# Block sums of the weights of the last projection: adding DMAs from memory instead of VectorE

## What is computed

```python
def swiglu_ffn(h, w_ffn_in, w_ffn_out):
    gate, up = jnp.split(h @ w_ffn_in, 2, axis=-1)
    return (jax.nn.silu(gate) * up) @ w_ffn_out
```

## Time and profile before

| what | value |
|---|---|
| device time, median of 3 runs | 1336.9 us (1336.31 to 1337.07) |
| span of the profiled execution | 1334.3 us |
| PE busy | 1314.1 us, 98% of the span |
| DVE busy | 983.0 us, 74% |
| ACT busy | 553.2 us, 41% |
| granted PE clock, mean | 0.998 of full speed |
| weight loads (SP) | 119 of 1024 KB, 5.0 us from issue to landing in the middle |

### The profile page before, as it was taken

How to read it: one execution, slowest core, us unless ns; L and a number is a source line. 1 busy time by engine, 2 the same in 40 slices (tenths; PEclk the granted TensorE clock), 3 DMA queues, 4 the chain that set the end, 5 groups by cost and what they waited for, 6 DMA issues and landing times.

```text
span 1334.3 us, 15752 instructions
## 1 busy us (share of the span) xinstructions
PE 1314.1 (98%) x6395; PEld 1065.0 (80%) x6395; DVE 983.0 (74%) x1218; ACT 553.2 (41%) x767; POOL 87.9 (7%) x153
## 2 busy tenths in 40 slices
PE   7999999999999999999999999999999999999997
PEld 4799688778888888888788777778878888888886
DVE  4787877989778777777759799866795444446988
ACT  4553444344333333232332566774443222224543
POOL 0000000000001000100000011000002120000001
PEclk9999999999999999999999999999999999999999
DMA  9543056325455556654232211122204333225565
GB/s 391 195 136 133 4 170 207 125 81 187 158 173 176 183 162 206 221 203 163 87 106 95 88 65 46 56 95 95 95 32 156 115 116 105 98 103 199 192 221 195
DMA packets 34472, 188.01 MB, mean 141 GB/s; under 512 B 4304, under 2 KB 5088, under 8 KB 18016
## 3 DMA queue, kind: packets, MB, share of 16 engines
q1 hardware_dynamic: 20976, 140.32, 29.7%
q0 software_dynamic: 13424, 46.69, 11.0%
HBM read 182.79 MB, written 4.20 MB: 140 GB/s over the span
## 4 chain that ended last, share of the span: by engine, by line
PE 84%; DVE 8%; ACT 3%; DMA 3%; issue 2%; SPq 0%; DVEq 0%; ACTq 0%
PE bank L1678 25%; PE bank L1680 24%; PE bank L1679 24%; PE bank L2017 2%; PE bank L2018 2%; PE bank L2023 2%; DVE WL L938 2%; DMA raw<-weights 1%; PE bank L1883 1%; DMA adaf<-ada 1%; DVE ada_acc L980 1%; PE bank L2213 1%; ACT WH L448 1%; PE bank L2183 1%; PE bank L2201 1%
## 5 line engine op out<-in xcount | busy, mean ns | idle before, releaser
L1678 PE MATMUL bank<-hH,WH 128*128 128x512 f32 x992 | 390.1, 393 | 0.8 <-DVE WL L938 0.5
L1680 PE MATMUL bank<-hH,WL 128*128 128x512 f32 x992 | 386.4, 390 | 0.0
L1679 PE MATMUL bank<-hL,WH 128*128 128x512 f32 x992 | 386.2, 389 | 0.0
L938 DVE TENSOR_TENSOR WL<-raw,WH 128x2048 fp32r<-128x2048 f32 (+1 forms) x114 | 253.5, 2226 | 153.9 <-ACT WH L448 153.9
L448 ACT ACTIVATE WH<-raw 128x2048 fp32r<-128x2048 f32 (+1 forms) x117 | 218.0, 1865 | 237.4 <-DMA raw<-weights 180.0
L1678 PEld LDWEIGHTS bank<-hH,WH 128*128 128x128 f32 x992 | 186.3, 188 | 42.6 <-issue 3.3
L1680 PEld LDWEIGHTS bank<-hH,WL 128*128 128x128 f32 x992 | 186.2, 188 | 39.2
L1679 PEld LDWEIGHTS bank<-hL,WH 128*128 128x128 f32 x992 | 186.4, 188 | 37.7 <-issue 0.2
L980 DVE SCALAR_TENSOR_TENSOR ada_acc<-ada_half,csil,ada_acc 128x1024 f32<-128x1024 f32 x70 | 89.6, 1280 | 5.6 <-DMA ada_half<-ada_later 3.0
L1427 DVE SCALAR_TENSOR_TENSOR cacc<-uT,vec,cacc 128x511 f32<-128x511 f32 (+29 forms) x120 | 83.2, 753 | 0.0
L401 POOL DMA_DIRECT2D ada_half<-ada_later x80 | 42.4, 530 | 570.7 <-DVE ada_acc L980 335.1
(11 more groups left out here) (358 smaller groups left out, 2147.3 us busy)
## 6 DMA issues: line engine op xcount, KB each, us to landing
raw<-weights SPq DMA_DIRECT2D x119, 1024.0 KB, 5.0
ada_half<-ada_later POOLq DMA_DIRECT2D x80, 512.0 KB, 4.5
adaf<-ada SPq DMA_DIRECT2D x8, 1024.0 KB, 19.9
xT<-x_t SPq DMA_DIRECT2D x4, 512.0 KB, 5.8
x_rows<-xB POOLq DMA_DIRECT2D x32, 64.0 KB, 2.2
gF<-x_rows POOLq DMA_DIRECT2D x3, 512.0 KB, 6.9
ctxT<-ctx_t SPq DMA_DIRECT2D x1, 1024.0 KB, 28.3
out_t<-gF SPq DMA_DIRECT2D x2, 512.0 KB, 2.6
```

The source lines that it names most:

```text
L938: TT_(lo_of(c, 0, width), raw_of(c, 0, width), hi_of(c, 0, width), sub).then_inc(s.lo_done, 1)
L1678: mm(o, lh, rh, start=start, stop=False, skip_group_check=skip)
L1679: mm(o, lh, rl, start=False, stop=False, skip_group_check=skip)
L1680: return mm(o, ll, rh, start=False, stop=stop, skip_group_check=skip)
```

## The change

The block sums that are plain additions move into DMAs that POOL issues. Such a DMA reads weights from memory and adds them to what lies in the `raw` tile (`accum_op=add`).

- First pass: A21 += A22 is now such a DMA of 256 KB (`add_block`). A12 = A11 - A22 stays on DVE.
- Second pass: SP loads only the first three blocks, 768 KB. A21 += A11 is a DMA of 256 KB, and A11 += A12 with A12 += A22 is one of 512 KB (`add_rows`). DVE does no sums here.
- POOL issues a chunk's adds once its load has landed and the adds of the chunk two before have landed. ACT's `split_hi` waits for the adds (semaphores `ada_in`), and in the first pass for DVE's difference as well.
- The adds stand on POOL ahead of the four `x_rows` loads.

```diff
+def added_up_to(c):
+    return 16 * (STEPS // 2 + sum(1 if x < C_REST else 2 for x in range(C_DOWN2, c + 1) if (x - c) % 2 == 0))
...
             def load_chunk(c):
                 sp.wait_ge(s.mm_done, 16 * freed_by(c) + 16)
-                sp.dma_start(raw_of(c), weights[c if c < C_REST else c - PAIRED]).then_inc(raw_in[slot_of(c)], 16)
+                if c < C_REST:
+                    sp.dma_start(raw_of(c), weights[c]).then_inc(raw_in[slot_of(c)], 16)
+                else:
+                    sp.dma_start(raw_of(c, 0, 3 * CW), weights[c - PAIRED, :, 0:3 * CW]).then_inc(raw_in[slot_of(c)], 16)
...
+            def add_block(c, to, of):
+                pool.dma_start(raw_of(c, CW * to, CW * to + CW), weights[c if c < C_REST else c - PAIRED, :, CW * of:CW * of + CW],
+                               accum_op=add).then_inc(ada_in[c % 2], 16)
+
+            def add_rows(c):
+                src = weights[c - PAIRED, :, CW * W_A12:CW * W_A22 + CW].rearrange("p (b j) -> p b j", j=CW)
+                pool.dma_start(quarters(c, 0, 3, 2), src, accum_op=add).then_inc(ada_in[c % 2], 16)
+
+            for c in range(C_DOWN2, N_LOADS):
+                pool.wait_ge(raw_in[slot_of(c)], 16 * loads_up_to(c))
+                if c >= C_DOWN2 + 2:
+                    pool.wait_ge(ada_in[c % 2], added_up_to(c - 2))
+                if c < C_REST:
+                    add_block(c, W_A21, W_A22)
+                else:
+                    add_block(c, W_A21, W_A11)
+                    add_rows(c)
             pool.wait_ge(s.mm_done, 16 * freed_by(N_LOADS - 1) + 16)
...
             def split_hi(c, width=CH):
                 if c >= C_DOWN2:
-                    act.wait_ge(s.w_sum, 2 * (c - C_DOWN2) + 2)
+                    if c < C_REST:
+                        act.wait_ge(s.w_sum, c - C_DOWN2 + 1)
+                    act.wait_ge(ada_in[c % 2], added_up_to(c))
...
             def weight_sums(c):
                 dve.wait_ge(raw_in[slot_of(c)], 16 * loads_up_to(c))
-                a11, a21 = raw_of(c, CW * W_A11, CW * W_A11 + CW), raw_of(c, CW * W_A21, CW * W_A21 + CW)
-                a12, a22 = raw_of(c, CW * W_A12, CW * W_A12 + CW), raw_of(c, CW * W_A22, CW * W_A22 + CW)
-                if c < C_REST:
-                    TT_(a21, a21, a22, add).then_inc(s.w_sum, 1)
-                    TT_(a12, a11, a22, sub).then_inc(s.w_sum, 1)
-                else:
-                    TT_(a21, a21, a11, add).then_inc(s.w_sum, 1)
-                    dve.wait_ge(s.w_sum, 2 * (c - C_DOWN2) + 1)
-                    TT_(quarters(c, 0, 3, 2), quarters(c, 0, 3, 2), quarters(c, 2, 4), add).then_inc(s.w_sum, 1)
+                a11, a12 = raw_of(c, CW * W_A11, CW * W_A11 + CW), raw_of(c, CW * W_A12, CW * W_A12 + CW)
+                TT_(a12, a11, raw_of(c, CW * W_A22, CW * W_A22 + CW), sub).then_inc(s.w_sum, 1)
...
-                if c + 1 < N_LOADS:
+                if c + 1 < C_REST:
                     weight_sums(c + 1)
```

## The result

| | before | changed |
|---|---|---|
| device time, median of the runs | 1336.6 us (1335.2 to 1337.1) | 1410.8 us (1410.0 to 1412.9, 4 runs) |
| span of the profiled execution | 1334.3 us | 1408.6 us |
| ratio to before, 95% interval | | 1.0557 (1.0542 to 1.0572) |
| mean granted PE clock | 0.998 | 0.976 |

The forecast was 1347.1, its range ended at 1362. The kernel is 74 us slower, where 10 were forecast. First the page of the changed kernel, the lines that answer to the earlier trace rows. PE has more busy time and yet a smaller share of the span; DVE has 25.7 us less to do; ACT waits for DMAs.

A forecast was written before the change was run, and what follows sets the result against it. PE, busy 98% of the span, was taken as the bound. Costs of 2.8 + 4.7 + 2.7 = 10.2 us moved the span from 1334.3 to 1344.5; the median, 2.6 above, gave 1347.1 us, range 1337 to 1362.

The forecast's parts named there:

- The ceiling: Most the change could gain: PE's three late starts, 1.95 us, plus at most 0.7 after PE's last matmul, 2.65 us.
- what is removed: DVE's block sums in both passes, 28.7 us, nearly all beside PE, so worth only what PE loses.
- What is added: Latency ahead of ACT's rounding: adds at the pace of POOL's plain loads, 3.9 us for 256 KB, 4.5 for 512 KB.
- the high end: Upper estimate at each place, with adds taking the engines twice as long for their bytes: +4.0, +7.3 and +5 us.
- the adds take twice their bytes: Rival: two reads per write, 5.55 us of DMA engines a second-pass chunk against PE's 4.08; 1358 us, chance 0.25.
- Place 1: Entry of the first pass: chunk 2's add lands at 1229.5, so PE starts that chunk 2.8 us later.
- The last up tile: At the first pass's entry: its silu and product slip by 2.6 us, hidden from PE with 0.2 in hand.
- Place 2: Where the passes meet: second-pass chunk 2's adds land at 1281.0, so PE starts the pass 4.7 us later.
- Place 3: Rest of the second pass and tail: a chunk's data just fit; late last chunk and row loads cost 2.7 us.
- Worse than that: Rival: adding packets wait for their reads of `raw`; at three times the bytes 7.4 us a chunk, 1375 and above, chance 0.10.

The follow-up runs named there:

- plain: The changed kernel with the same DMAs of the same bytes as plain copies, nothing added: 1362.8 us, ratio 1.0194.
- ring2k: The changed kernel with 2048 instead of 1024 bytes per partition for POOL's DMA descriptors: 1385.9 us, ratio 1.0367.

## Why the prediction was wrong, point by point

**The ceiling** was right: 2.65 forecast, 2.1 measured with the sums left out. So was **what is removed**: the rows of the three lines that are gone add up to 28.7 us. DVE's busy time fell by only 25.7, because it counts each moment once, and back to back rows of DVE overlap by about 0.1 us, 33 times. It brought nothing.

**What is added** is where it failed first. "I take an add at this pace", the pace of POOL's plain loads, 3.9 for 256 KB and 4.5 for 512. The first figure was right for an add by itself (4.0) and for the middle of all 22 (4.8). The second was not: 8.7 in the middle. The working took loads of another kind as the nearest rows and put the two reads into the high end only. It also read 426 GB/s as the pace of POOL's loads; the stretch of the earlier trace rows has SP's alone. POOL's copy of 256 KB took 0.91 us of the engines in `plain`, not the 0.6 that every sum uses. The rival "the adds take twice their bytes" had this right in kind and nearly in size: 1.55 against 0.91 us alone. For a chunk it said 5.55 us of the engines; 6.65 were measured.

**Place 1.** +2.8 forecast, at most 4.0; 7.7 measured. The step that failed is "4.5, so it lands at 1229.5". The add of chunk 2 was issued at 1225.56, 0.6 later than forecast, and landed 8.8 us later, at 1234.4. From there to PE were 4.3 us, as worked out. So 4.3 of the 4.9 us missed are the landing. The copy in the same place took 7.7 us to land where the add took 8.8, and PE waited 6.8 us for it instead of 6.9. What was mis-sized is the 0.6 for two loads still flowing: in the ten us from 1225 on POOL's queue got little more than a quarter of the engines, as the section on the hardware shows. So this place was decided by the queueing beside SP's loads, which no rival had as a mechanism. The last up tile, called "hidden, with only 0.2 in hand", did cost PE 0.4 us, on `gF` at L1597, but that vanished in the longer wait behind it.

**Place 2.** +4.7 forecast, 7.3 as its high end; the stretch that ends there gave 20.4 on top of place 1, 1.9 of it as slow clock in the first pass and 18.5 as PE's wait. The step that failed is "POOL issues the adds at 1274.7". The load was issued at 1279.0, 9.6 later than in the earlier trace rows, of which 7.7 is place 1 and 1.9 the slow clock behind it, and landed at 1286.2. With the latencies forecast its adds would have landed 6.4 later, at 1292.6. They were issued at 1295.49, 9.3 us after the landing, because the room for POOL's descriptors was full, and landed at 1304.3. Beyond the forecast's own 4.7 and the 1.9 these are 13.7 us: 2.0 for the load, which took 7.2 instead of 5.2, 9.2 for the room, and 2.5 for adds that took 8.8 instead of 6.3. `ring2k` takes only 4 us of the wait away: there the load took 7.6 us, the 512 KB add of chunk 2 was still held by the room for 4.3, and the one of chunk 1 that held it took 12.3 to land.

**Place 3.** "3.7 us of data in PE's 4.08. It just fits" is the costliest sentence of the prediction: 44.4 of the 74. The data took 6.65 us, and the room made it worse: one chunk's adds at a time, from issue to landing, gives 9 to 12 us a chunk, 10.0 in the mean of ten. So PE waited 29.0 us in seven places, and its clock fell with the waits. The tail had the forecast's wait: DVE waits for the residual rows at `row_bias` (L1650) before the row that ends the program.

```profile
1392.60 0.21 DVE L1650 TENSOR_SCALAR ybias<-ysum 128x1 f32<-128x1 f32 x2 [2.69 <-DMA gF<-x_rows]
...
1404.08 1.41 DVE L1663 SCALAR_TENSOR_TENSOR gF<-gained,yscale,gF 128x512 f32<-128x512 f32 x2
```

From 1392.60 to 1404.08 is 11.5 us, as from 1318.46 to the last row before. But the room had a part in this too: POOL stood 6.7 us before the second of the four row loads, until the last 512 KB add had landed. Against PE's last matmul the end is 1.9 us later; the forecast's 2.7 held 1.7 of PE's own, so it had 1.0 here.

**The rivals.** "Worse than that", with 7.4 us a chunk and 1375 and above, came nearest to the time, and in part for a reason that it didn't have: the engines' own pace is 6.65 us, and the room made 10.0 of it. Its 0.10 was too little, and so was the 0.25 of the two reads: the prediction itself said of it that "nothing in the trace speaks against it", while for the forecast's own pace there was no row of an add either. The range left the worst case out. Half the way to the forecast's high ends (16.3 us in all) is 1350.2, not 1352, which changes nothing here. **The clock** had no term at all: every sum took PE at 0.227 us a matmul, also behind a stand of many us.

What stays open: how the 49 us left in `ring2k` divide. With the engines at 0.88 their pace is a large part, but POOL still stood 21 us for room, and a run with 4096 was not made. And why chunk 5's 512 KB add needed 12.4 us alone in its kernel, where the eleven of the changed kernel needed 8.3 to 11.6. SP's loads come closer together there, since PE is not held up, but no run separates it.

## What to carry to other kernels

An add by DMA stands behind the load that it adds to and costs more engine time than the load of as many bytes (here 1.7 times a copy's). So ask first for slack of two latencies as they are beside other transfers (here 4 to 12 us for an add, 5 to 9 for a load), and only then for idle bandwidth. Before giving POOL DMAs to issue in a stream, look whether it idles before one of them without a semaphore: the room for its descriptors may hold no more than one step's transfers. And work taken off an engine beside the critical path is worth only the waits that PE loses by it: 2.1 us here, with 32.6 us of DVE's work left out.

## What the runs showed of the hardware

**POOL stalls in a DMA issue when its descriptors have no room**, and no semaphore shows it: 80.9 us in ten waits with 1024 bytes, each ending 0.2 to 0.3 us after the landing of the 512 KB add ahead, and none of them ahead of L436 with 2048.

**A DMA of POOL's doesn't get half of the engines beside SP's loads.** From 1225 to 1235 in the changed kernel (queue, packets, MB, share):

```profile
q1 hardware_dynamic: 393, 2.83, 72.0%
q0 software_dynamic: 252, 0.48, 28.2%
```

and with copies:

```profile
q1 hardware_dynamic: 474, 3.49, 85.1%
q0 software_dynamic: 160, 0.52, 15.0%
```

Chunk 2's add, issued at 1225.56, took 8.8 us, and the copy in its place 7.7, against 4.0 and 3.2 alone. POOL's packets are the smaller ones: 0.48 MB in 252 against 2.83 MB in 393. The Trainium skill, "DMA: Bandwidth & Descriptors", section "Anatomy of one DMA — SWDGE (gpsimd) path", gives 2.0 us plus the bytes at 436 GB/s. By this page 256 KB take an estimated 2.6 us. The measured 3.2 alone and 7.7 beside SP's loads are both longer, and the measurement decides.

**PE's waits cost a third more than their length in this kernel**: 18.1 us of extra busy time came with 54 us more of waits. The granted clock was 0.80 to 0.50 in the stretches shown that hold waits, and 0.86 in the one behind the first, in which PE was busy throughout. It did not fall everywhere alike: from 1320 to 1340 PE was busy for 12.3 of 20 us, and the clock was 0.96.
